# A parity-ordered copy of transposed X for the value chunks of the dilated groups

## The reference, cut to what matters

```
proj = x @ w_in
attn_qkv, ret_q, ret_k, ret_v, ret_g, gate_a, gate_r = split(proj)
# 3 attention groups (window, dilation): (128, 1), (512, 4), (2048, 16)
...
scores = einsum('brhnqd,brhnkd->brhnqk', qb, kc) * (dh ** -0.5)
out = einsum('brhnqk,brhnkd->brhnqd', softmax(mask(scores)), vc)
```

## Time and profile before

| | us |
|---|---|
| median of 3 runs | 1483.27 |
| lowest and highest run | 1483.08, 1483.8 |
| profiled execution | 1483.36 |
| its span, first to last instruction | 1481.6 |
| TensorE busy, matmuls | 1470.9 (99%) |
| VectorE busy | 1017.1 (69%) |
| ScalarE busy | 785.2 (53%) |
| GpSimd busy | 46.0 (3%) |

### The profile page before, as it was taken

One profiled execution on the slowest core, in us unless ns is written; L12 is line 12 of the kernel. 1 busy time (PEld: TensorE's weight loads), 2 busy tenths in 40 slices (PEclk: granted clock), 3 DMA queues, 4 the chain that ended last, 5 costly groups with the idle time before them and its releaser, 6 DMA issues.

```text
span 1481.6 us, 20356 instructions
## 1 busy us (share of the span) xinstructions
PE 1470.9 (99%) x8370; PEld 1292.8 (87%) x8370; DVE 1017.1 (69%) x1165; ACT 785.2 (53%) x845; POOL 46.0 (3%) x30
## 2 busy tenths in 40 slices
PE   9999999999999999999999999999999999999998
PEld 8888898888888888888888888888888888888886
DVE  6775665756755688777866656667566556887777
ACT  5564454554744456566544545546446444566562
POOL 0000000000000020000010000000000000100000
PEclk9999999999999999999999999999999999999999
DMA  9645446445456565655555555454545565665560
GB/s 315 230 149 171 150 157 201 147 165 168 152 183 216 184 209 177 210 198 198 173 171 169 169 171 162 151 191 151 170 148 184 179 206 177 202 220 178 180 237 37
DMA packets 232621, 266.86 MB, mean 180 GB/s; under 512 B 4320, under 2 KB 222944, under 8 KB 231904
## 3 DMA queue, kind: packets, MB, share of 16 engines
q1 hardware_dynamic: 231312, 264.57, 53.9%
q10 hardware_dynamic: 1232, 1.18, 0.3%
HBM read 264.68 MB, written 1.05 MB: 179 GB/s over the span
## 4 chain that ended last, share of the span: by engine, by line
PE 97%; DVE 1%; ACT 1%; DMA 0%; issue 0%; ACTq 0%; DVEq 0%
PE bank L1336 39%; PE bank L1341 21%; PE bank L1322 7%; PE bank L1324 7%; PE bank L1323 7%; PE acc L1322 4%; PE acc L1323 4%; PE acc L1324 4%; PE acc L1508 1%; PE acc L1485 1%; PE acc L1463 1%; PE acc L1481 1%; PE bank L1374 1%; DMA scratch<-xT 0%; PE acc L1470 0%; PE acc L1528 0%
## 5 line engine op out<-in xcount | busy, mean ns | idle before, releaser
L774 DVE TENSOR_TENSOR w_lo<-raw,w_hi 128x2048 fp32r<-128x2048 f32 x234 | 535.6, 2290 | 262.3 <-ACT w_hi L405 261.9
L405 ACT ACTIVATE w_hi<-raw 128x2048 fp32r<-128x2048 f32 x241 | 459.7, 1909 | 148.2 <-PE bank L1324 80.1
L1336 PE MATMUL bank<-xT_both,w_hi 128*128 128x512 f32 x2208 | 528.3, 391 | 0.0
L1336 PEld LDWEIGHTS bank<-xT_both,w_hi 128*128 128x128 f32 x2208 | 407.4, 188 | 80.9 <-DVE mid_lo L1024 0.4
L1341 PEld LDWEIGHTS bank<-xT_both,w_lo 128*128 128x128 f32 x2208 | 283.1, 191 | 10.7
L1341 PE MATMUL bank<-xT_both,w_lo 128*128 128x256 f32 x2208 | 286.4, 283 | 0.0
L525 ACT ACTIVATE scratch<-bank 128x512 f32<-128x512 f32 x80 | 47.9, 598 | 229.9 <-PE bank L1341 229.9
L1322 PE MATMUL bank<-w_hi,xT_both 128*128 128x512 f32 (+1 forms) x464 | 162.1, 349 | 0.4 <-DVE xT_both L842 0.3
L1324 PE MATMUL bank<-w_hi,xT_both 128*128 128x512 f32 (+1 forms) x464 | 160.9, 347 | 0.0
L1323 PE MATMUL bank<-w_lo,xT_both 128*128 128x512 f32 (+1 forms) x464 | 160.8, 347 | 0.0
L1184 DVE SCALAR_TENSOR_TENSOR scratch<-scratch,feat 128x256 f32<-128x256 f32 x176 | 77.4, 481 | 33.7 <-ACT scratch L684 28.8
(11 more groups left out here) (173 smaller groups left out, 1385.0 us busy)
## 6 DMA issues: line engine op xcount, KB each, us to landing
raw<-w_in SPq DMA_DIRECT2D x133, 1024.0 KB, 5.1
raw<-w_up SPq DMA_DIRECT2D x44, 1024.0 KB, 5.1
raw<-w_down SPq DMA_DIRECT2D x20, 1024.0 KB, 5.1
raw<-w_ret_proj SPq DMA_DIRECT2D x16, 1024.0 KB, 5.2
raw<-w_attn_proj SPq DMA_DIRECT2D x8, 1024.0 KB, 5.3
raw<-w_out SPq DMA_DIRECT2D x8, 1024.0 KB, 4.9
raw<-w_ple_gate SPq DMA_DIRECT2D x8, 1024.0 KB, 5.1
scratch<-ln_rows SPq DMA_DIRECT2D x4, 1024.0 KB, 7.3
```

The costliest lines, as they stand in the source:

```text
L405: nc.scalar.activation(w_hi[:, s, :], raw[:, s, :], ACT.Copy).then_inc(hi_ready, 1)
L774: nc.vector.tensor_tensor(w_lo[:, s, :], raw[:, s, :], w_hi[:, s, :].bitcast(F32), ALU.subtract).then_inc(lo_ready, 1)
L1336: mm(pair[p][:, m, :], hi[:, o:o + P], src[:, k0 + k, :, :].rearrange("p a t -> p (a t)"), start=first and k == 0, stop=False)
```

## The change

ScalarE gets a new routine, `by_parity(k)`, called in the first iteration (j = 0) of each layer after the work of each chunk c = 3 to 10, with k = c - 3. For the high and for the low part of X it copies block k to another place with the even tokens ahead of the odd ones. The places are rows 8 to 11 (high) and rows 4 to 7 (low) of ret. Each call counts one on the new semaphore `turned`. TensorE waits for 8 counts per layer before the pair v12 when j < 3. `two_chunks` takes the parts of X as an argument: for the pair v12 it reads the high part from the copy for j = 0, 1, 2 and the low part from the copy for j = 0, 1, by contiguous tiles, and otherwise X itself by every second token, as before.

```diff
+        turned_lo = ret[:, 4:8, :, :].rearrange("p a b t -> p (a b) t")
+        turned_hi = ret[:, 8:12, :, :].rearrange("p a b t -> p (a b) t")
...
+        turned = sem("turned")
...
+                def by_parity(k):
+
+                    for x, dst in ((xT_hi, turned_hi), (xT_lo, turned_lo)):
+                        ins = nc.scalar.activation(dst[:, k, :].rearrange("p (r m) -> p r m", r=2),
+                                                   x[:, k, :].rearrange("p (m r) -> p r m", r=2), ACT.Copy)
+                    ins.then_inc(turned, 1)
+
...
                     if c in (4, 5):
                         near_high(c - 4)
+                    if j == 0 and c in range(3, 11):
+                        by_parity(c - 3)
                     if c == 10:
                         exp(0)
...
-            def two_chunks(l, c, b, t, ks=range(KT), every_second=False):
-
-                def tokens(x, k):
-                    return x[:, k, t:SEQ:2] if every_second else x[:, k, t * P:(t + 1) * P]
+            def two_chunks(l, c, b, t, ks=range(KT), x_parts=(xT_hi, xT_lo), every_second=(False, False)):
+
+                def tokens(i, k):
+                    return x_parts[i][:, k, t:SEQ:2] if every_second[i] else x_parts[i][:, k, t * P:(t + 1) * P]
...
-                                        tokens(xT_hi, k), tokens(xT_lo, k),
+                                        tokens(0, k), tokens(1, k),
...
                         weights_ready(g, c + 1)
-                        two_chunks(l, c, bank_of(c), 0, every_second=c == v12)
+                        if c == v12 and j < NJ - 1:
+                            pe.wait_ge(turned, KT * (l + 1))
+                        if c == rv:
+                            x_parts, every_second = (xT_hi, xT_lo), (False, False)
+                        else:
+                            x_parts = (turned_hi if j < 3 else xT_hi, turned_lo if j < 2 else xT_lo)
+                            every_second = (j >= 3, j >= 2)
+                        two_chunks(l, c, bank_of(c), 0, range(KT), x_parts, every_second)
                         bank_free(c + 1)
-                        two_chunks(l, c, bank_of(c + 1), 1, every_second=c == v12)
+                        two_chunks(l, c, bank_of(c + 1), 1, range(KT), x_parts, every_second)
```

## The result

The changed kernel took 1485.29 us (median of 22 runs, 1484.89 to 1485.8), the kernel before, on the same chips, 1483.18 (22 runs, 1482.89 to 1483.96). That is 2.11 us more, a ratio of 1.0014 with a 95% interval of 1.0008 to 1.002: slower beyond the interval, and inside the 0.2% that counts as no change. The prediction said 1485.1.

What follows compares the result with a forecast made beforehand. TensorE, busy for 99% of the span, was taken as the bound. From 1483.36 us, a gain of 1.44 from contiguous loads and a loss of 3.1 from waits were summed to 1485.1 us, range 1483.6 to 1486.9.

Steps and rivals of the forecast that it cites:

- What bounds the kernel: Whole span: TensorE, busy 99%, is the bound; every wait it newly gets is lost in full.
- The sum: Whole kernel: 1483.36 - 1.44 + 3.1 = 1485.1 us, 0.1% more, which counts as no change.
- Part 3: TensorE before c = 11, j = 0: waits for the last copies, 1.56 us lost a layer, 3.1 us in two.
- the sine and cosine: ScalarE rows of the same shape, 0.42 and 0.40 us, starting 0.32 apart, taken as the copies' cost.
- Part 2: ScalarE, chunks 3 to 10 of j = 0: copies hidden but for the last; weights' high part 0.65 us later.
- Part 1: Pairs at c = 11: contiguous weight loads save 6.7 ns a step, 0.27 us a full pair, 1.44 us in all.
- My bound from below: Pair of j = 2: gains nothing if one strided load in three holds up its neighbours; total gain then 1.08 us.
- (a): Pairs at c = 11: the stride costs nothing, only the stalls are left, 1486.5 us; chance 12%.
- (b): Start of c = 11, both layers: TensorE's clock falls in the new gaps, 1.8 us each, 1488.7 us; chance 6%.
- (c): Wait before c = 11: costs nothing, the last count being there already; gain alone left, 1481.9 us; chance 6%.

Runs made afterwards that it cites:

- the wait alone: The change with copies and wait kept, but all pairs of groups 1 and 2 reading X by every second token: 1486.55 us, ratio 1.0021 to before.
- the copies alone: The change with its copies kept, but no wait on them and all pairs reading X by every second token: 1483.29 us, ratio 0.9999 to before.
- the early versions: The change with copies ahead of each chunk's copy out, 1482.18 us; or only k = 7's moved to chunk 9, 1482.31; or early copies plus low part in attn, 1481.83.
- stride four: Early-copies version with both copies, but weight loads of the j = 0 to 2 pairs take every fourth element of X: 1484.42 us, ratio 1.0007 to before.

## Why the prediction was right

**What bounds the kernel** held: TensorE had no idle time that could take the new wait in, and the run with the wait alone lost it in full.

**The sum.** Its terms make 1483.36 - 1.44 + 3.1 = 1485.0, not 1485.1. As a difference that is +1.7 us where +2.1 was measured: 0.34 us of the gain did not come, and the waits cost 0.04 more. That the forecast stands only 0.2 us below the measured 1485.29 is in part luck, since it was built on an execution of 1483.36 and the runs beside the change have a median of 1483.18.

**Part 3, the wait,** was worked out as 1.56 us a layer and was 1.58. Each term can be held against its row: successor after the copy out 0.49 predicted, 0.50 measured; the two parity copies 0.72 and 0.74; ScalarE to TensorE 0.15 and 0.14. Taking the sine and cosine as the nearest rows was the right choice: reading every second element and writing fp32r together cost ScalarE 0.02 us in two copies. What it left out is the restart: 0.08 us more over the pair's first seven steps. The same 1.70 us stand in the earlier trace rows, where transposes and no stop come before the pair, so a slow first step (0.31 us and not 0.23) isn't peculiar to a stop.

**Part 2, the hidden copies,** held: the copies alone left the time as it was. VectorE's rows in the changed kernel, for the low parts of chunks 11 and 12, show the delay of the high part and its cover:

```profile
61.23 2.29 DVE L786 TENSOR_TENSOR w_lo<-raw,w_hi 128x2048 fp32r<-128x2048 f32 x1 [1.75 <-ACT w_hi L408]
...
67.55 2.29 DVE L786 TENSOR_TENSOR w_lo<-raw,w_hi 128x2048 fp32r<-128x2048 f32 x1
```

For chunk 11 VectorE waited 1.75 us and not 1.11, so the high part came 0.64 us later, where 0.65 was predicted; for chunk 12 it had no wait, since it came from its rotation.

**Part 1, the gain,** has the source right and one size wrong: 1.44 predicted, 1.1 measured. The full pairs of j = 1 gained 0.27 and 0.28 as worked out; those of j = 0 lost 0.08 of it to the restart. The mis-sized term is the pair of j = 2. I gave it two thirds of the gain, 0.18 us, because two thirds of its loads became contiguous, and it gained 0.09 (steps of 231 ns, not 229). The cost isn't in proportion to the strided loads: the first in three already costs 4.4 of the 6.7 ns. My bound from below, nothing for j = 2, held it.

**The rivals.** (a), the stride costs nothing, falls with 10.91 against 11.19 us for the same pair with the same neighbours, in the early versions and in j = 1 of the change. The rule of the Trainium skill behind it (SBUF — State Buffer, Door 1: The DMA port swizzle), that elements four bytes wide and two apart are free, isn't borne out at 188 against 193 ns, and the 6.7 ns a step. Its line of 16 bytes fits what stride four did, 310 ns, but the same passage names four fp32 elements as a stride that is free, and that these 310 ns contradict. (b), the clock: the granted clock is 0.999 over the span as before, and 1.00 from 72.33 to 84, the level of 2.4 GHz, and the products after each gap stand 0.23 us apart behind a first step of 0.31, not 0.4. A gap of 1.4 us without a matmul left the pace as it was. (c), a wait that costs nothing, is what the change would be with its last two copies elsewhere, 0.94 to 1.13 us faster than before (1.4 expected).

## What to carry to other kernels

When a helper engine prepares an operand, ask which instruction of its own queue the last piece stands behind: here seven eighths of the copies were free, and the last cost 3 us because it was queued behind a result of the very engine that then waited for it. Moving that call by a few lines turned a loss of 2.1 us into a gain of 1.1 on the medians, though a gain of that size is under 0.1% and its interval just touches no change. And count a saving per stage from the steps of the stage itself: at j = 2 two thirds of the loads became cheaper, and that was one third of the gain.

## What the runs showed of the hardware that I had not expected

A TensorE weight load of 128 columns took 188 ns contiguous, 193 at a stride of two float32 elements and 310 at a stride of four, while the step of its 512-column product went only from 226.7 to 233.3 to 235.0 ns. One strided load in three gave 231.1 whichever of the three it was, and two gave 233.2. Why the first of three costs two thirds of the whole is not settled; no run here looks into the overlap of a load with the product before it, and the durations don't tell, since the load of 310 ns is longer than the step of 235. Where TensorE came to a pair c = 11 without a stop, its first seven steps were the same with and without the stride of two (1.61 to 1.63 us; 1.76 at stride four), so by these rows a run of seven such products or fewer would gain nothing from contiguous operands; no experiment tried one.
